# Probabilities times values in three passes of split parts, and VectorE's program woven unit by unit, in two attentions

## The chip, the cores and the metric

The kernel runs on one core of a Trainium2 chip. The metric is the device time of one execution in microseconds (us). A program has five engines that run their own instruction lists and meet at semaphores: TensorE (PE in the rows, with its weight loads as PEld), VectorE (DVE), ScalarE (ACT), GpSimd (POOL), and SyncE (SP), which only issues transfers here.

## The reference

Two transformer-like blocks run one after the other over 1024 tokens of width 1024. The change touches only their two attentions. In the first block ("fox") there are 8 heads of width 64 over 1040 positions (16 learnt ones ahead of the tokens), a causal mask and a bias per key:

```
s = jnp.einsum('bhqd,bhkd->bhqk', qi, kh, preferred_element_type=jnp.float32) * scale
s = s + Fi[..., None] - F[:, :, None, :]
s = jnp.where(kpos[None, :] <= pi[:, None], s, -jnp.inf)
p = jax.nn.softmax(s, axis=-1)
return jnp.einsum('bhqk,bhkd->bhqd', p.astype(vh.dtype), vh)
```

In the second ("mla") there are 16 heads with queries and keys of width 96 and values of width 64 over 1024 positions, and a mask by chunks of 64:

```
s = jnp.einsum('bqhd,bkhd->bhqk', qb, k[:, :k_end]).astype(jnp.float32) * scale
s = jnp.where(mask, s, -jnp.inf)
p = jax.nn.softmax(s, axis=-1).astype(v.dtype)
outs.append(jnp.einsum('bhqk,bkhd->bqhd', p, v[:, :k_end]))
```

Everything is float32. Around the attentions stand projections, a pooling and a convolution mixer, a recurrent branch and two mixtures of experts, which take most of the time and are left as they are.

## The kernel before, in words

Both attentions are the function `attention` (L976). A head is cut into **units**: one unit is 128 keys against up to 512 queries of one half of the sequence. The mla attention has 12 units a head: 512, 384, 256 and 128 queries for half 0, then five of 512 and 384, 256, 128 for half 1. The fox attention has 14: 512, 400, 272, 144, 16 for half 0, then five of 512 and 400, 272, 144, 16. For u, the number of the unit in its head, every engine has its own list.

**TensorE** holds two units of scores ahead. Its loop does, per unit u, the scores of u + 2 (L122: three products of split parts, high by high, low by high, high by low, with the mask added at L1189), then two pieces of the next head's row maxima (L1161, mask at L1164) while u is small, and last the product of unit u with the values, `fox_out` or `mla_out` (L1202). That product has float32 operands; the others have operands of the type fp32r, which are the rounded parts of a float32 number: the high part is a rounded copy, the low part is the value less the high part. The scores have three banks (R_S), the probabilities three buffers (R_P), the maxima two banks (R_M). At the head's first unit TensorE waits for the row of maxima, the copied values and the low parts.

**ScalarE** takes the exponential of every unit (L1257), copies finished sums out (L1245, after unit 1 for the half before and two units after the end of half 0), and after unit 7 (HIGH_AT) makes the high parts of the queries and keys of the head after next (L1239, two casts).

**VectorE** works head by head: it reduces all of the next head's maxima (L1276), joins and negates them (L1281), copies the turned row (L1285), inverts sums (L1064) and scales finished halves (L1069). The scaling reads two tensors in on-chip memory (SBUF); the inverse sums come to it by a transfer to DRAM and a spreading transfer back, both issued by SyncE (`inverse_of`).

**GpSimd** makes the low parts of queries and keys (L1131, two subtractions of 1024 or 1040 columns) once the scores of the head two before are done, and copies the values of a head to a buffer with a column of ones (L1123, one copy for each 128 keys).

**SyncE** loads the queries and keys of head h + 2 when the low parts of head h are there, and moves the sums, the inverses and the row of maxima. `Handover` (L957) holds the buffers that the stage behind the attention uses too.

## Time and profile before

| | us |
|---|---|
| median of 3 runs | 2957.4 |
| lowest, highest | 2955.4, 2964.36 |
| the profiled execution, its own time | 2955.65 |
| its span in the profile | 2953.9 |
| fox attention, from its first memory fill to its last copy out | 306.6 to 492.4 |
| mla attention, the same | 1668.7 to 1991.2 |

The two attentions are some 510 us of the span. Over the whole span TensorE is busy for 2664.0 us (90%), VectorE 1490.2 (50%), ScalarE 1113.5 (38%) and GpSimd 812.7 (28%). In the rows each operation has its line in the kernel before, its output and inputs, and its shape; "idle before" is the time its engine stood still ahead of it and what ended that. A TensorE record's duration overlaps with the next one's, so what a product costs is read from the distance between starts.

### The profile page before, as it was taken

To read this page: it belongs to the slowest core of one execution; us is meant where nothing else is said; L and a number is where in the kernel's file an instruction comes from. 1 tells how busy PE (TensorE), PEld (TensorE's weight loads), DVE (VectorE), ACT (ScalarE), POOL (GpSimd) and SP (SyncE) were. 2 spreads that over 40 slices of the span, in tenths; PEclk is the share of its full clock that TensorE was granted. 3 is DMA by queue.
4 is the path that set the end of the run, shared out by engine and by line. 5 is a ranking of instruction groups with operands and counts; after the bars stand their busy time and mean duration, and the time that the engine had idled before them with its cause. 6 is when DMAs were issued, how large, how long until landed. Compare 5 with 4: busy or idle time off the path is not lost. (4 is left out here: it accounts for less than half of the span.)

```text
span 2953.9 us, 34232 instructions
## 1 busy us (share of the span) xinstructions
PE 2664.0 (90%) x12244; PEld 2034.3 (69%) x12244; DVE 1490.2 (50%) x1840; ACT 1113.5 (38%) x1461; POOL 812.7 (28%) x685
## 2 busy tenths in 40 slices
PE   4999899999999799958999799999999989699887
PEld 3899566677668677746777455557777868677665
DVE  4196342222123578855466544433542443677775
ACT  3011443000012377752344344441332232377775
POOL 1242332212122133312100233323332312134444
PEclk7999899999999799978899899999999999799998
DMA  3110112111105487842522233332111123598985
GB/s 95 30 50 22 33 43 63 43 43 50 36 22 179 170 286 231 273 131 86 213 64 65 75 84 75 74 86 67 50 36 50 50 94 123 194 329 305 320 321 185
DMA packets 209415, 350.52 MB, mean 119 GB/s; under 512 B 40376, under 2 KB 159496, under 8 KB 189608
## 3 DMA queue, kind: packets, MB, share of 16 engines
q1 hardware_dynamic: 191824, 315.60, 32.0%
q0 software_dynamic: 17280, 33.60, 4.9%
q8 instruction: 56, 0.92, 0.1%
q14 instruction: 39, 0.32, 0.0%
q10 hardware_dynamic: 216, 0.07, 0.0%
HBM read 326.80 MB, written 72.48 MB: 135 GB/s over the span
## 5 line engine op out<-in xcount | busy, mean ns | idle before, releaser
L2078 DVE TENSOR_TENSOR moe_run_w_low_up<-moe_run_w,moe_run_w_high_up 128x2048 fp32r<-128x2048 f32 x116 | 265.4, 2289 | 127.7 <-ACT moe_run_w_high_up L1911 118.6
L1911 ACT CAST moe_run_w_high_up<-moe_run_w 128x2048 fp32r<-128x2048 f32 x116 | 221.2, 1906 | 114.1 <-DMA moe_run_w<-w_gate 63.9
L1848 PE MATMUL moe_run_up<-moe_run_w_high_up,moe_run_xT_high 128*128 128x512 f32 x464 | 192.6, 415 | 14.0 <-issue 13.7
L1848 PE MATMUL moe_run_up<-moe_run_w_low_up,moe_run_xT_high 128*128 128x512 f32 x464 | 184.0, 397 | 0.0
L1848 PE MATMUL moe_run_up<-moe_run_w_high_up,moe_run_xT_low 128*128 128x512 f32 x464 | 183.9, 396 | 0.0
L1394 DVE TENSOR_TENSOR merge_gated<-merge_branch,merge_gate 128x512 f32<-128x512 f32 x48 | 33.2, 691 | 280.9 <-ACT merge_gate L1378 280.7
L1257 ACT ACTIVATE mla_probs<-mla_scores 128x512 f32<-128x512 f32 x192 | 94.1, 490 | 174.6 <-PE mla_scores L1189 91.6
L1378 ACT ACTIVATE merge_gate<-merge_gates 128x512 f32<-128x512 f32 x48 | 28.7, 598 | 347.2 <-PE merge_branch L122 347.2
L1202 PE MATMUL mla_out<-mla_probs,mla_v 128*65 128x512 f32 (+3 forms) x384 | 150.4, 487 | 0.0
L134 PE MATMUL moe_run_down<-moe_run_w_high_down,moe_run_hT_high 128*128 128x512 f32 x232 | 98.3, 424 | 39.7 <-issue 36.0
L2078 DVE TENSOR_TENSOR moe_run_w_low_down<-moe_run_w,moe_run_w_high_down 128x2048 fp32r<-128x2048 f32 x58 | 132.3, 2281 | 0.0
L1276 DVE TENSOR_REDUCE mla_piece_max<-mla_max 128x1 f32<-128x512 f32 (+1 forms) x192 | 98.9, 550 | 60.4 <-PE mla_max L1161 41.2
L1848 PEld LDWEIGHTS moe_run_up<-moe_run_w_high_up,moe_run_xT_high 128*128 128x128 f32 x464 | 88.1, 190 | 46.5 <-issue 29.4
L122 PE MATMUL merge_branch<-features,merge_wy 128*128 128x512 f32 x256 | 117.7, 592 | 0.0
L134 PE MATMUL merge_gates<-uT_high,merge_wg_high 128*128 128x512 f32 x256 | 113.7, 444 | 0.0
L1918 ACT CAST moe_run_w_high_down<-moe_run_w 128x2048 fp32r<-128x2048 f32 x58 | 110.4, 1903 | 1.2 <-DMA moe_run_w<-exp_w 0.6
L1766 POOL DMA_INDIRECT out<-moe_run_y,moe_run_rows x34 | 58.3, 1715 | 179.8 <-DMA out<-moe_run_y,moe_run_rows 137.8
L134 PE MATMUL rnn_ps<-uT_again_high,mla_q_hi_then_high 128*128 128x512 f32 x256 | 102.2, 399 | 5.4 <-ACTq L2233 5.4
L1756 POOL DMA_INDIRECT moe_run_x<-v,moe_run_rows x58 | 91.7, 1580 | 49.9 <-POOL moe_run_rows L1792 44.8
L134 PE MATMUL proj_acc<-uT_high,proj_w_high 128*128 128x512 f32 (+2 forms) x272 | 97.1, 357 | 8.3 <-DVEq L559 8.2
L1848 PEld LDWEIGHTS moe_run_up<-moe_run_w_high_up,moe_run_xT_low 128*128 128x128 f32 x464 | 87.7, 189 | 21.2
L134 PE MATMUL rnn_ps<-uT_again_high,rnn_w_high 128*128 128x512 f32 x256 | 101.2, 396 | 0.0
(556 smaller groups left out, 7401.2 us busy)
## 6 DMA issues: line engine op xcount, KB each, us to landing
moe_run_w<-exp_w SPq DMA_DIRECT2D x72, 1024.0 KB
moe_run_w<-w_gate SPq DMA_DIRECT2D x34, 1024.0 KB
moe_run_w<-w_up SPq DMA_DIRECT2D x34, 1024.0 KB
moe_run_w<-w_down SPq DMA_DIRECT2D x34, 1024.0 KB
out_h<-x SPq DMA_DIRECT2D x16, 512.0 KB, 4.5
v<-out_v SPq DMA_DIRECT2D x16, 512.0 KB, 2.9
mla_raw_q_then_weights<-w_in SPq DMA_DIRECT2D x16, 512.0 KB, 3.9
rnn_raw<-w_in SPq DMA_DIRECT2D x16, 512.0 KB
```

The source lines that it names most:

```text
L122: last = pe.matmul(out, lhsT, rhs, start=(n == 0), stop=(n == len(pairs) - 1))
L134: last = pe.matmul(out, a, b, start=(k == 0), stop=(k == n - 1))
L1202: pe.matmul(ps_o[n][0:DH + 1, first - a:b - a], v_aug[h % 2][0:rows, t, :], probs[g % R_P][0:rows, first - a:b - a], start=(t == 0), stop= ...
L1257: act.activation(probs[g % R_P][0:rows, first - a:b - a], ps_s[g % R_S][0:rows, first - a:b - a], ACT.Exp).then_inc(s_exp, 1)
L1276: dve.tensor_reduce(pm[:, i, n:n + 1], ps_m[g % R_M][:, 0:b - a], AX.X, ALU.max).then_inc(s_mxfree, 1)
L1394: dve.tensor_tensor(pr[b][:], ps_y[b][:], sg[b][:], ALU.mult).then_inc(s_done, 1)
L1756: pool.indirect_dma_start(out=x[p][:], out_offset=None, in_=v_d, in_offset=bass.IndirectOffsetOnAxis(ap=rows[p][:, 1:2], axis=0), bounds_c ...
L1766: pool.indirect_dma_start(out=h_d, out_offset=bass.IndirectOffsetOnAxis(ap=rows[p][:, 0:1], axis=0), in_=y[p][:], in_offset=None, bounds_c ...
L1848: last = pe.matmul(up[p][:], a, w, start=(h == 0 and k == 0), stop=(h == 1 and k == 3 * HK - 1))
L1911: act.copy(hi[p][j], raw[p][j][:]).then_inc(s_hi[j], 1)
L1918: act.copy(hi[p][2], raw[p][2][:]).then_inc(s_hi[2], 1)
L2078: dve.tensor_tensor(lo[p][j], raw[p][j][:], hi[p][j].bitcast(F32), ALU.subtract).then_inc(s_lo[j], 1)
```

## The change

The product of probabilities and values is made in three passes of split parts, as the scores are.

- Values: GpSimd makes `v_hi` (a cast) and `v_lo` (a subtraction) for a head, each over all tiles at once, in place of 8 or 9 copies.
- Probabilities: behind every exponential ScalarE waits for it and makes `probs_hi`; VectorE then makes `probs_lo`, which lies over `probs` (`over`: two names for one place). TensorE waits for the first before its first two passes and for the second before its third.
- Queries and keys: the low part lies over the raw part. There are three such buffers, used in turn. GpSimd makes a head's low parts as soon as ScalarE has made the high ones; it no longer waits for the scores of an earlier head. ScalarE makes the high part of the queries after unit 7 and of the keys after unit 9.
- VectorE's list is woven: in each unit first `probs_lo`, then two maxima of the next head, and at set units the joining, the turned row, the inverses and the scalings.
- The constant rows are filled by VectorE (`s_const`), zeros in the low rows by GpSimd; SyncE waits for the scores of the head before in place of the low parts.

```diff
-    HIGH_AT = 7
-    INV1_AT = NM // 2
+    HIGH_AT = (7, 9)
+    LAST_MAX = FIRST + -(-NM // PER_UNIT) - 1
+    SCALE0_AT, INV1_AT, SCALE1_AT, INV0_AT = 1, 3, 8, ends[0] + 6
...
-                        sp.wait_ge(s_lo, 2 * h + 2)
-                        load_head(sp, p, h // 2 + 1, raw[p][0], raw[p][1], s_load[p])
+                        if h:
+                            sp.wait_ge(s_sc, NU * h)
+                        else:
+                            sp.wait_ge(s_init, 3)
+                        load(h + 2)
...
+                def split_v(h):
                     if h >= 2:
                         pool.wait_ge(s_pv, NU * (h - 1))
-                    for t in range(NK):
-                        rows = min(P, T - P * t)
-                        last = pool.tensor_copy(v_aug[h % 2][0:rows, t, 0:DH], v[0:rows, t, h * DH:(h + 1) * DH])
+                    high, low = v_hi[h % 2], v_lo[h % 2]
+                    for rows, tiles in ((P, slice(0, full)),) + (((rest, slice(full, NK)),) if rest else ()):
+                        src = v[0:rows, tiles, h * DH:(h + 1) * DH]
+                        own(pool.tensor_copy(high[0:rows, tiles, 0:DH], src))
+                        last = pool.tensor_tensor(low[0:rows, tiles, 0:DH], src,
+                                                  high[0:rows, tiles, 0:DH].bitcast(F32), ALU.subtract)
                     last.then_inc(s_v[h % 2], 1)
 
                 def split_low(h):
-                    if h >= 2:
-                        pool.wait_ge(s_sc, NU * (h - 1))
-                    for n, rows in enumerate((one_row, k_all)):
+                    for n, rows in enumerate((dq, one_row)):
                         pool.wait_ge(s_hi, 2 * h + n + 1)
...
-                    pe.wait_ge(s_exp, g + 1)
-                    pe.matmul(ps_o[n][0:DH + 1, first - a:b - a], v_aug[h % 2][0:rows, t, :],
-                              probs[g % R_P][0:rows, first - a:b - a],
-                              start=(t == 0), stop=True, skip_group_check=True).then_inc(s_pv, 1)
+                    pe.wait_ge(s_ph, g + 1)
+                    out, at = ps_o[n][0:DH + 1, first - a:b - a], slice(first - a, b - a)
+                    vh, vl = (w[h % 2][0:rows, t, :] for w in (v_hi, v_lo))
+                    ph, pl = (w[g % R_P][0:rows, at] for w in (p_hi, p_lo))
+                    pe.matmul(out, vh, ph, start=(t == 0), stop=False, skip_group_check=True)
+                    pe.matmul(out, vl, ph, start=False, stop=False, skip_group_check=True)
+                    pe.wait_ge(s_pl, g + 1)
+                    pe.matmul(out, vh, pl, start=False, stop=True, skip_group_check=True).then_inc(s_pv, 1)
...
                                        ps_s[g % R_S][0:rows, first - a:b - a], ACT.Exp).then_inc(s_exp, 1)
+                        act.wait_ge(s_exp, g + 1)
+                        act.copy(p_hi[g % R_P][0:rows, first - a:b - a],
+                                 probs[g % R_P][0:rows, first - a:b - a]).then_inc(s_ph, 1)
...
-                        if u == HIGH_AT and h + 2 < heads:
-                            split_high(h + 2)
+                        if u in HIGH_AT and h + 2 < heads:
+                            split_high(h + 2, HIGH_AT.index(u))
...
+                def rest_of_probs(h, u):
...
+                    dve.wait_ge(s_ph, g + 1)
+                    dve.tensor_tensor(p_lo[g % R_P][0:rows, first - a:b - a], probs[g % R_P][0:rows, first - a:b - a],
+                                      p_hi[g % R_P][0:rows, first - a:b - a].bitcast(F32),
+                                      ALU.subtract).then_inc(s_pl, 1)
...
                 for h in range(heads):
-                    if h + 1 < heads:
-                        maxima_of(h + 1)
-                    else:
-                        invert(dve, h - 1, 1)
-                    if h:
-                        scale_out(dve, h - 1, 1)
-                    invert(dve, h, 0)
-                    scale_out(dve, h, 0)
+                    for u in range(NU):
+                        rest_of_probs(h, u)
+                        if h + 1 < heads:
+                            for m in range(PER_UNIT * (u - FIRST), PER_UNIT * (u - FIRST + 1)):
+                                if 0 <= m < NM:
+                                    max_of(h + 1, m)
```

VectorE's list in an mla head was, before (`mla_sums` are the sums to be inverted, `oT` the finished output):

```order
L1276 TENSOR_REDUCE mla_piece_max<-mla_max 128x1 x7
L1064 RECIPROCAL mla_sums<-mla_sums 128x4
L1276 TENSOR_REDUCE mla_piece_max<-mla_max 128x1 x5
L1281 TENSOR_REDUCE mla_neg_max<-mla_piece_max 128x8
L1285 CAST mla_neg_rows<-mla_turned 8x128
L1069 TENSOR_TENSOR oT<-mla_unscaled,oT 64x512
L1064 RECIPROCAL mla_sums<-mla_sums 128x4
L1069 TENSOR_TENSOR oT<-mla_unscaled,oT 64x512
```

The last row stood ahead of the next head's maxima. From unit 5 to the end of the head VectorE's list is now this (`mla_probs_lo` with a number of its own for each of the three buffers):

```order
L1315 TENSOR_TENSOR mla_probs_lo_11617<-mla_probs,mla_probs_hi 128x512
L1296 TENSOR_REDUCE mla_piece_max<-mla_max 128x1 x2
L1301 TENSOR_REDUCE mla_neg_max<-mla_piece_max 128x8
L1315 TENSOR_TENSOR mla_probs_lo_11615<-mla_probs,mla_probs_hi 128x512
L1315 TENSOR_TENSOR mla_probs_lo_11616<-mla_probs,mla_probs_hi 128x512
L1307 CAST mla_neg_rows<-mla_turned 8x128
L1315 TENSOR_TENSOR mla_probs_lo_11617<-mla_probs,mla_probs_hi 128x512
L1078 TENSOR_TENSOR oT<-mla_unscaled,oT 64x512
L1315 TENSOR_TENSOR mla_probs_lo_11615<-mla_probs,mla_probs_hi 128x384
L1073 RECIPROCAL mla_sums<-mla_sums 128x4
L1315 TENSOR_TENSOR mla_probs_lo_11616<-mla_probs,mla_probs_hi 128x256
L1315 TENSOR_TENSOR mla_probs_lo_11617<-mla_probs,mla_probs_hi 128x128
```

A subtraction stands in every unit, and the scaling of half 1 in unit 8; the scaling of half 0 moved to unit 1 of the next head.

ScalarE's list in an mla head, from unit 7 on, before:

```order
L1257 ACTIVATE mla_probs1<-mla_scores1 128x512
L1239 CAST mla_q_hi_then_high<-mla_raw_q_then_weights 96x1024
L1239 CAST mla_k_hi_then_low<-mla_k0 97x1024
L1257 ACTIVATE mla_probs2<-mla_scores2 128x512
L1257 ACTIVATE mla_probs0<-mla_scores0 128x384
L1257 ACTIVATE mla_probs1<-mla_scores1 128x256
L1257 ACTIVATE mla_probs2<-mla_scores2 128x128
```

The same place in the changed program:

```order
L1274 ACTIVATE mla_probs1<-mla_scores1 128x512
L1277 CAST mla_probs_hi1<-mla_probs1 128x512
L1254 CAST mla_q_hi_then_high<-mla_q2 96x1024
L1274 ACTIVATE mla_probs2<-mla_scores2 128x512
L1277 CAST mla_probs_hi2<-mla_probs2 128x512
L1274 ACTIVATE mla_probs0<-mla_scores0 128x384
L1277 CAST mla_probs_hi0<-mla_probs0 128x384
L1254 CAST mla_k_hi_then_low<-mla_k2 96x1024
L1274 ACTIVATE mla_probs1<-mla_scores1 128x256
L1277 CAST mla_probs_hi1<-mla_probs1 128x256
L1274 ACTIVATE mla_probs2<-mla_scores2 128x128
L1277 CAST mla_probs_hi2<-mla_probs2 128x128
```

Every exponential has a cast behind it, and the cast of the keys moved to behind unit 9. GpSimd's subtractions of the same head are issued right behind these two casts, in units 7 to 11, and its list for a head is now:

```order
L1147 TENSOR_TENSOR mla_q_lo2_11613<-mla_q2,mla_q_hi_then_high 96x1024
L1147 TENSOR_TENSOR mla_k_lo2_11614<-mla_k2,mla_k_hi_then_low 96x1024
L1139 CAST mla_v_hi0<-v2_tokens 128x8x64
L1140 TENSOR_TENSOR mla_v_lo0<-v2_tokens,mla_v_hi0 128x8x64
L1147 TENSOR_TENSOR mla_q_lo0_11610<-mla_q0,mla_q_hi0 96x1024
```

Before, the first two rows ran at the start of a head, behind the scores of the head before, and eight copies stood in place of the third and fourth.

## Rows read from the trace of the kernel before

**Rows 1.** Busy time of each engine in three stretches of one head: fox, mla, mla
```profile
core 0: us, PE busy (x) PEld busy (x) DVE busy (x) ACT busy (x) POOL busy (x), PEclk, DMA share, GB/s
344.30:365.20 20.90, 20.14 (x106) 12.86 (x104) 9.73 (x19) 9.14 (x19) 6.78 (x11) 1.00 0.17 39
1762.30:1781.70 19.40, 18.38 (x90) 11.37 (x89) 8.32 (x18) 8.60 (x17) 6.59 (x10) 1.00 0.37 109
1744.30:1763.37 19.07, 18.35 (x90) 11.36 (x89) 8.03 (x18) 8.64 (x17) 6.57 (x11) 1.00 0.28 57
```
**Rows 2.** Timeline of TensorE in an mla head: start us, us, operation
```profile
1764.66 0.40 PE L122 MATMUL mla_scores<-mla_q_lo,mla_k_hi 97*128 97x512 f32 x1
1764.89 0.40 PE L122 MATMUL mla_scores<-mla_q_hi,mla_k_lo 97*128 97x512 f32 x1
...
1778.45 1.02 PE L1202 MATMUL mla_out<-mla_probs,mla_v 128*65 128x512 f32 x2
1778.91 0.74 PE L122 MATMUL mla_scores<-mla_q_hi,mla_k_hi 97*128 97x384 f32 x1
1779.48 0.34 PE L122 MATMUL mla_scores<-mla_q_lo,mla_k_hi 97*128 97x384 f32 x1
1779.66 0.34 PE L122 MATMUL mla_scores<-mla_q_hi,mla_k_lo 97*128 97x384 f32 x1
```
**Rows 3.** Waits of TensorE for VectorE, mla then fox: us, times, longest
```profile
PE mla_max L1161 <- DVE mla_piece_max L1276: 11.4, 14, 1.0
PE fox_max L1161 <- DVE fox_piece_max L1276: 5.0, 6, 0.9
```
**Rows 4.** Groups of ScalarE by shape: exponentials and casts, busy us, mean ns
```profile
L1257 ACT ACTIVATE mla_probs<-mla_scores 128x512 f32<-128x512 f32 x87 | 51.9, 596 | 105.3 <-PE mla_scores L122 75.2 <-PE mla_scores L1189 28.5
L1257 ACT ACTIVATE mla_probs<-mla_scores 128x384 f32<-128x384 f32 x30 | 14.7, 490 | 11.0 <-PE mla_scores L1189 10.2
L1239 ACT CAST mla_k_hi<-mla_k 97x1024 fp32r<-97x1024 f32 x9 | 9.4, 1045 | 0.0
L398 ACT CAST uT_high<-norm_turn 128x512 fp32r<-128x512 f32 x32 | 17.6, 579 | 6.1 <-PE norm_turn L460 5.9
```
**Rows 5.** Groups of VectorE by shape: maxima, fox scalings, two-input operations elsewhere
```profile
L1276 DVE TENSOR_REDUCE mla_piece_max<-mla_max 128x1 f32<-128x512 f32 x86 | 57.9, 688 | 38.4 <-PE mla_max L1161 38.4
L1069 DVE TENSOR_TENSOR features<-fox_unscaled,features 64x512 f32<-64x512 f32 x14 | 19.0, 1359 | 44.0 <-DMA features<-fox_inverse 43.9
L447 DVE TENSOR_TENSOR uT_low<-norm_turn,uT_high 128x512 fp32r<-128x512 f32 x32 | 20.7, 683 | 1.6 <-ACT uT_high L398 1.6
L2657 DVE TENSOR_TENSOR qkv_q<-qkv_q,latent_squares 128x256 f32<-128x256 f32 x8 | 3.4, 425 | 0.3
```
**Rows 6.** Timeline of GpSimd and VectorE: the scaling beside GpSimd's subtraction, and alone
```profile
455.75 2.42 POOL L1131 TENSOR_TENSOR fox_k_lo<-fox_k,fox_k_hi 66x1040 fp32r<-66x1040 f32 x1
455.85 2.87 DVE L1069 TENSOR_TENSOR features<-fox_unscaled,features 64x512 f32<-64x512 f32 x1 [4.92 <-DMA features<-fox_inverse]
...
1785.10 2.36 POOL L1131 TENSOR_TENSOR mla_k_lo<-mla_k,mla_k_hi 97x1024 fp32r<-97x1024 f32 x1
1786.73 1.28 DVE L1069 TENSOR_TENSOR oT<-mla_unscaled,oT 64x512 f32<-64x512 f32 x1 [5.30 <-DMA oT<-mla_inverse]
...
1799.46 0.67 DVE L1069 TENSOR_TENSOR oT<-mla_unscaled,oT 64x512 f32<-64x512 f32 x1
```
**Rows 7.** Groups of GpSimd: subtractions in mla and in the recurrent branch, copied values
```profile
L1131 POOL TENSOR_TENSOR mla_k_lo<-mla_k,mla_k_hi 97x1024 fp32r<-97x1024 f32 x9 | 21.2, 2361 | 0.0
L147 POOL TENSOR_TENSOR rnn_w_low<-rnn_raw,rnn_w_high 128x1024 fp32r<-128x1024 f32 x16 | 49.7, 3106 | 1.3
L1123 POOL COPY mla_v<-v_tokens 128x64 f32<-128x64 f32 x112 | 27.2, 291 | 0.0
```
**Rows 8.** Timeline from an inverse to its scaling: VectorE, SyncE's issue, VectorE
```profile
1761.62 0.16 DVE L1064 RECIPROCAL mla_sums<-mla_sums 128x4 f32<-128x4 f32 x1
1763.37 0.47 SPq L1059 DMA_DIRECT2D oT<-mla_inverse  x1
1767.99 0.80 DVE L1069 TENSOR_TENSOR oT<-mla_unscaled,oT 64x512 f32<-64x512 f32 x1 [6.22 <-DMA oT<-mla_inverse]
```
**Rows 9.** Busy time in stretches of 20 us in the expert stages, columns as in rows 1
```profile
1140.00:1160.00 20.00, 16.51 (x65) 12.88 (x64) 14.80 (x12) 11.82 (x11) 6.04 (x5) 0.83 0.80 263
2820.00:2840.00 20.00, 16.53 (x73) 12.44 (x73) 15.55 (x12) 13.61 (x13) 8.69 (x6) 1.00 0.91 324
```

137 lines of the change are left out of this document (86 added, 51 removed).

## The prediction

> **What bounds the kernel now.** I first cut one head out of each attention and read each engine's busy time [rows 1]. A fox head takes 20.9 us, an mla head 19.07 or 19.40, 19.2 in the mean. TensorE is busy for all but about 1 us of it, with the granted clock at 1.00; ScalarE and VectorE work 8 to 10 us of 19 to 21, GpSimd under 7. So TensorE's list sets a head's length. The one hole in it is a wait of up to 1.0 us a head for a bank of maxima [rows 3]: VectorE stands at the scaling of a finished half, whose inverse is still on its way [rows 8], and the maxima are queued behind it. The change takes work from TensorE and puts new work on the three others; the question is whether TensorE still sets the pace.
>
> **TensorE.** From the timeline [rows 2]: a pass of 512 fp32r columns starts 0.23 us after the last (1764.66 to 1764.89), one of 384 after 0.18. The float32 product of 512 columns starts at 1778.45; the scores behind it reach their second pass at 1779.48, so their first, of 0.18, ran from 1779.30, and the product held the array 0.85 us. Three passes take 3 x 0.233 = 0.70: 0.15 saved on each of 6 units of 512, 0.1 and 0.07 on the two units each of 384 and 256, and about 0.1 lost on the two of 128, where three passes of about 0.1 (weight loads set them) replace 0.21. That is 0.9 + 0.2 + 0.14 - 0.2 = 1.05 us less in an mla head, and by the same count 0.8 in a fox head. With the wait of rows 3 gone too (0.8 us a head in either), TensorE alone would need about 17.4 us for mla and 19.3 for fox.
>
> On this point the Trainium skill can be weighed against the row. FP8 and Floating Point Precision, section TensorE Precision Notes, says that true FP32 takes four passes through the array. The 0.85 us are four times 512 columns at the granted full clock, so it agrees; by it, with passes of equal length, the saving would be 0.21 for a unit of 512 and some 7 us more over all 24 heads than I count. The row's 0.233 for an fp32r pass decides.
>
> **ScalarE.** An exponential of 512 columns is 0.60 us, of 384 0.49 [rows 4], by their slope 0.39 for 256 and 0.28 for 128: 5.9 us an mla head. The cast behind each is not in the trace in that shape. From on-chip memory 1024 columns take 1.045, and 512 columns from a bank 0.579 [rows 4]; I take 0.60, 0.49, 0.39, 0.28, another 5.9 us. With two copies out (0.58 each) and two casts of queries and keys (1.04 each) the list is 15.05 us, and 0.5 for the waits on itself (12 x 0.04, an estimate): 15.5. It can start 1.06 us into the head (first scores 0.83, handover 0.23) and I count 1.5 us in which it waits for scores, because TensorE stands two units ahead at most. It ends at 18.1; the last subtraction of 128 columns (0.29), two passes and their handovers bring the head to **19.0 us**. That is 0.2 under 19.2. For fox the same list (12.7 + 3.2 + 0.6 us) gives **20.2**, 0.7 under 20.9. So even undisturbed most of what TensorE saves is lost, at the end of each head, where exponential, cast, subtraction and product of four narrowing units stand in a row and the next head's scores are queued behind the last product.
>
> **VectorE.** The subtraction is bounded by 0.683 us (512 columns, one input from a bank) and by 0.425 for 256 from on-chip memory [rows 5]: 0.69, 0.56, 0.43, 0.29, some 0.07 less when back to back, some 6 us an mla head. A maximum of 512 is 0.69, all twelve 5.9. From the first subtraction's end (3.0 us into the head) VectorE needs for units 0 to 6: maxima 5.9, subtractions 3.6, one scaling 0.65, joining and inverse 0.3, with small waits for banks to 13.4 us, where TensorE would want unit 6 at about 13.2. So it is level until there.
>
> **GpSimd, the term that decides.** Look at the scaling, the one VectorE operation before with both inputs in on-chip memory [rows 6]. Alone it takes 0.67 us. At 455.85 it meets GpSimd's subtraction (455.75 to 458.17) and takes 2.87: it ends 0.55 after GpSimd. At 1786.73 it meets one that ends at 1787.46 and ends 0.55 after that. It stands still until GpSimd is through. The fourteen fox scalings of that stretch take 1.36 us in the mean [rows 5]; every second one meets GpSimd. `probs_lo` has the same form, and there are 12 or 14 a head. The other way round GpSimd waits too: its subtraction, 2.36 alone, takes 3.11 in the recurrent branch [rows 7]. Before, the two subtractions of 2.36 us stood at a head's start, and met one scaling. Now they follow the casts behind units 7 and 9, where VectorE has no maxima left and TensorE waits for each subtraction.
>
> A head of mla, laid out in that way: the cast of the queries ends at 13.2 (ScalarE's list to unit 7). GpSimd waits for unit 6's subtraction to end at 13.4, then holds until 15.8. Unit 7's is through at 16.4; TensorE wanted it at 14.9. The keys' cast ends at 16.6 and GpSimd takes its second 2.4 us at once or one operation later; either way VectorE then has to fit 2.4 of waiting, unit 8 (0.62), the scaling (0.65), unit 9 (0.5), the inverse (0.15), unit 10 (0.4) and unit 11 (0.28) behind 16.4: 21.4, and with the last pass **21.7 us**, +2.5 on 19.2. Fox: 16.3 + 2.4 + 0.62 + 0.65 + 0.62 + 0.15 + 1.42 (units 10 to 13) + 0.3 = **22.5**, +1.6 on 20.9. The last two heads of each attention have no such casts. The values' cast and subtraction (some 1.9 us from rows 7's rates, against 8 x 0.29 of copies) run at a head's start, before the first subtraction, and cost nothing unless the head before ran late.
>
> The same rule stands in the Trainium skill, SBUF - State Buffer, section SBUF: two separate sides: the port pair that VectorE and GpSimd share is held for a whole instruction, also between a VectorE operation with two SBUF inputs and a GpSimd one that reads SBUF, and the other blocks. By it the sum is the one below; read as mere sharing of bandwidth, rows 6 would give about half the delay, near 2976.
>
> **The small rest.** VectorE fills three rows (mla) or six (fox) before the first cast, unseen in the trace; the cast anyway waits some 6 us for its load: 0 to 3 us in all, I take 1. SyncE's loads wait for the same moment as before within 1 us and land ten units early: nothing. The last head's inverse is taken at unit 9 or 10 and needs 6.4 us to its scaling [rows 8], 1 us later than before for each attention: 2.
>
> **The sum.** 14 x 2.5 = 35.0, the two last mla heads -0.7, 6 x 1.6 = 9.6, the two last fox heads -1.4, and 3 of rest: +45.5 us. On the profiled execution's 2955.65 (span 2953.9, median of the runs 2957.4) that is 3001; I say 3002.
>
> **Rivals.**
> 1. Only one of GpSimd's two subtractions costs time, because the other falls beside maxima or an idle VectorE: about half the delay, 14 x 1.15, 6 x 0.5, less 2.1, and the 3 of rest: +20: 2976. For it: my layout puts the first only 0.5 us behind the last maxima.
> 2. GpSimd's share is hidden or VectorE wins the port: heads of 19.0 and 20.2, 16 x -0.2, 8 x -0.7, +3: 2950, on the edge of what can be told. Against it stand rows 6 and the fox mean of rows 5.
> 3. Faster: TensorE stays the bound, since casts and handovers are cheaper than I take them. Heads of 17.4 and 19.3: 16 x -1.8, 8 x -1.6, + 3: -39, 2917. It needs the four narrow units to follow each other within TensorE's own time; in units 10 and 11 one exponential, cast and subtraction come to 1.2 and 0.85 us against passes of 0.36 and 0.3, which speaks against it. It decides if ScalarE's list ends before 16.5 us.
> 4. Worse: with the inverse of half 0 taken at 21 us, its scaling (6.4 us later) is due 5.7 us into the next head, where VectorE comes to it at about 5.4; behind it maxima and subtractions stop. And TensorE would be busy under 80% of a head: at 16.5 of 20 us the granted clock was once 1.00 and once 0.83 [rows 9]. Either adds 1 us a head: 3026.
>
> **Chances.** Forecast 0.50, rival 1 0.14, rival 2 0.14, rival 3 0.14, rival 4 0.08. A difference under 0.3% (2948.5 to 2966.3) can't be told from none. Slower: 0.50 + 0.14 + 0.08 = 0.72; rival 2 straddles the edge, 0.09 same and 0.05 faster; with rival 3 faster is 0.19. The range takes in the forecast and rivals 1 and 2: 2942 to 3025, leaving 0.2 outside.
>
> **What would show it.** In the profile after: `probs_lo` of 512 columns with a median of 0.65 to 0.7 and a maximum near 3 us, the long ones in units 7 to 11; an mla head of 21 to 22 us with TensorE waiting for VectorE before the third pass; product passes 0.23 us apart; casts of 0.6. If no subtraction of probabilities is longer than 1 us, the deciding term is wrong; if heads are 19 us long, it was hidden.

## The result, and the profile after

The changed kernel takes 3047.3 us (median of 4 runs, 3044.5 to 3060.5; a fifth on record, outside that median, took 3039.5), the kernel before 2960.4 beside it: a ratio of 1.0296 [1.0261, 1.0331], 87 us more. Forecast were 3002, 45 more, and a range up to 3025. The sign and GpSimd's hold on VectorE were right. The price was half of what it is, because the sum had no term for TensorE's clock. The profiled execution is the slowest of the four, 3060.5, and 104.9 over the profiled one before, so its rows overstate the median by up to 13 us.

Busy time of each engine over the span of 3058.8 us, from the page of the changed kernel, and its row of the granted clock in 40 slices:

```profile
PE 2737.2 (89%) x12548; PEld 2123.3 (69%) x12548; DVE 1695.7 (55%) x2161; ACT 1256.7 (41%) x1765; POOL 860.7 (28%) x547
...
PEclk9999867999999799969899788879999999799999
```

The new work stands on VectorE (+205 us) and ScalarE (+143). TensorE, which was to lose work, is busy 73 us longer. A busy TensorE is not a fast one: in the 40 slices the clock row falls to 8, 6 and 7 inside fox (slices 5 to 7) and lies at 7 to 8 across mla (23 to 27).

From the first memory fill to the last copy out fox now takes 225.3 us (185.8 before) and mla 393.2 (322.5 before): +39.5 and +70.7, all of the loss; everything else together is 5 us shorter. The next view answers [rows 1]: busy time of each engine in stretches of the changed kernel, five fox heads in a row, two mla heads in a row, and a piece of the last mla head. Columns as there; the column after the POOL counts is the granted clock.

```profile
core 0: us, PE busy (x) PEld busy (x) DVE busy (x) ACT busy (x) POOL busy (x), PEclk, DMA share, GB/s
342.07:363.90 21.83, 19.46 (x119) 13.80 (x118) 16.68 (x34) 15.31 (x33) 7.07 (x6) 1.00 0.16 35
363.90:386.49 22.59, 20.75 (x118) 14.67 (x117) 17.07 (x35) 15.34 (x33) 7.06 (x7) 0.92 0.17 40
386.49:416.54 30.05, 27.25 (x112) 19.86 (x110) 17.35 (x34) 15.54 (x32) 7.08 (x6) 0.64 0.13 28
416.54:447.54 31.00, 29.87 (x118) 21.36 (x118) 16.85 (x35) 15.55 (x32) 8.56 (x7) 0.61 0.13 27
447.54:480.22 32.68, 30.39 (x118) 22.00 (x118) 16.94 (x35) 15.52 (x32) 7.45 (x7) 0.60 0.11 25
1789.20:1812.50 23.30, 20.43 (x102) 14.46 (x101) 17.10 (x31) 14.42 (x29) 7.16 (x4) 0.85 0.20 48
1812.50:1837.00 24.50, 21.72 (x102) 15.16 (x101) 17.20 (x32) 14.50 (x29) 7.15 (x5) 0.79 0.33 87
2075.00:2092.00 17.00, 16.71 (x93) 11.61 (x93) 9.77 (x21) 13.53 (x29) 0.00 (x0) 1.00 0.20 42
```

Read the fox rows downwards. VectorE, ScalarE and GpSimd have the same lists in every head. The first two heads take 21.8 and 22.6 us at clocks of 1.00 and 0.92, beside a forecast of 22.5. The next three take 30 to 33, with a clock near 0.6 and TensorE "busy" for all but 1 to 3 us. The mla heads are 23.3 and 24.5 in turn, 23.9 in the mean, at 0.85 and 0.79; forecast 21.7.

The timeline of GpSimd, VectorE and TensorE in one mla head shows how the two things hang together (start us, us, engine, line, operation; in brackets the wait before it). L1315 is `probs_lo`, L1147 GpSimd's subtraction, L1218 TensorE's third pass:

```profile
1789.21 2.93 POOL L1147 TENSOR_TENSOR mla_q_low<-mla_raw_q_then_weights,mla_q_hi 96x1024 fp32r<-96x1024 f32 x1 [14.19 <-ACT mla_q_hi L1254]
...
1790.73 1.97 DVE L1315 TENSOR_TENSOR mla_probs_lo<-mla_probs,mla_probs_hi 128x512 fp32r<-128x512 f32 x1
...
1792.47 2.44 POOL L1147 TENSOR_TENSOR mla_k_lo<-mla_k,mla_k_hi 96x1024 fp32r<-96x1024 f32 x1 [0.33 <-ACT mla_k_hi L1254]
1792.72 2.73 DVE L1078 TENSOR_TENSOR oT<-mla_unscaled,oT 64x512 f32<-64x512 f32 x1
...
1792.75 0.45 PE L1218 MATMUL mla_out<-mla_probs_lo,mla_v_hi 128*65 128x512 f32 x1 [0.67 <-DVE mla_probs_lo L1315]
...
1795.48 0.56 DVE L1315 TENSOR_TENSOR mla_probs_lo<-mla_probs,mla_probs_hi 128x384 fp32r<-128x384 f32 x1
...
1796.10 0.39 PE L1218 MATMUL mla_out<-mla_probs_lo,mla_v_hi 128*65 128x384 f32 x1 [2.19 <-DVE mla_probs_lo L1315]
```

GpSimd's first subtraction ends at 1792.14 and VectorE's at 1792.70; the second ends at 1794.91 and VectorE's scaling at 1795.45. Both times VectorE ends 0.55 us after GpSimd, the signature of [rows 6], twice in each head. The first hold costs TensorE 0.67 us. What was not in the forecast is that the long wait falls on the scaling: `probs_lo` of unit 9 is queued behind it and TensorE has a hole of 2.19 us. Then the clock answers. TensorE's passes behind that hole, and the clock in the two stretches:

```profile
1801.06 0.63 PE L1216 MATMUL mla_out<-mla_probs_hi,mla_v_lo 128*65 128x512 f32 x1
1801.49 0.63 PE L1218 MATMUL mla_out<-mla_probs_lo,mla_v_hi 128*65 128x512 f32 x1
...
1804.69 0.40 PE L122 MATMUL mla_scores<-mla_q_hi,mla_k_hi 97*128 97x512 f32 x1
1804.92 0.39 PE L122 MATMUL mla_scores<-mla_q_lo,mla_k_hi 97*128 97x512 f32 x1
```
```profile
1797.70:1804.60 6.90, 6.90 (x28) 5.22 (x28) 2.98 (x6) 3.91 (x9) 1.19 (x2) 0.51 0.50 136
1789.20:1797.70 8.50, 5.63 (x34) 3.73 (x34) 6.73 (x9) 4.26 (x9) 5.97 (x3) 1.00 0.03 6
```

Passes of 512 columns start 0.43 us apart and later 0.23 again: the lower level of the clock (1.2 GHz) and the upper (2.4). In the 8.5 us with the holes TensorE worked 5.63 at the full clock; the 6.9 us behind them ran at 0.51. In fox the lower level lasts longer, with TensorE busy throughout:

```profile
394.90:422.20 27.30, 27.30 (x97) 19.90 (x95) 12.29 (x28) 12.43 (x27) 4.63 (x5) 0.50 0.14 29
422.20:429.00 6.80, 5.67 (x38) 4.03 (x37) 4.84 (x8) 3.84 (x10) 4.31 (x2) 1.00 0.03 3
429.00:452.90 23.90, 23.90 (x81) 17.09 (x80) 12.01 (x26) 11.41 (x23) 4.25 (x5) 0.50 0.16 34
```

The groups by shape answer [rows 4] and [rows 5] (count, busy us, mean ns, idle before):

```profile
L1315 DVE TENSOR_TENSOR mla_probs_lo<-mla_probs,mla_probs_hi 128x512 fp32r<-128x512 f32 x96 | 82.0, 867 | 58.0 <-ACT mla_probs_hi L1277 58.0
L1277 ACT CAST mla_probs_hi<-mla_probs 128x512 fp32r<-128x512 f32 x96 | 59.6, 620 | 3.0
L1078 DVE TENSOR_TENSOR oT<-mla_unscaled,oT 64x512 f32<-64x512 f32 x32 | 49.9, 1560 | 8.6 <-DMA oT<-mla_inverse 8.0
```

The cast is 0.62 us (taken as 0.60). The subtraction has a mean of 0.87, against 0.69 in the sum, and the scaling 1.56, where it takes 0.67 alone.

### The profile page after: what moved, and what is told of

The parts are those of the page before. It is cut to its first block and busy times, and to the rows that moved or that the text cites. A ratio compares the mean times of both kernels' runs of the same rounds, so it can differ in the third digit from the quotient of the medians.

```text
span 3058.8 us, 35307 instructions
## 1 busy us (share of the span) xinstructions
PE 2737.2 (89%) x12548; PEld 2123.3 (69%) x12548; DVE 1695.7 (55%) x2161; ACT 1256.7 (41%) x1765; POOL 860.7 (28%) x547
## 5 line engine op out<-in xcount | busy, mean ns | idle before, releaser
L1902 PE MATMUL moe_run_up<-moe_run_w_high_up,moe_run_xT_high 128*128 128x512 f32 x464 | 193.5, 417 | 21.6 <-issue 21.4
L1315 DVE TENSOR_TENSOR mla_probs_lo<-mla_probs,mla_probs_hi 128x512 fp32r<-128x512 f32 x192 | 125.3, 665 | 58.9 <-ACT mla_probs_hi L1277 58.5
L1810 POOL DMA_INDIRECT moe_run_x<-v,moe_run_rows x58 | 115.8, 1996 | 50.2 <-POOL moe_run_rows L1846 37.2
L1218 PE MATMUL mla_out<-mla_probs_lo,mla_v_hi 128*65 128x512 f32 x192 | 74.7, 390 | 41.0 <-DVE mla_probs_lo L1315 40.7
L1902 PEld LDWEIGHTS moe_run_up<-moe_run_w_high_up,moe_run_xT_low 128*128 128x128 f32 x464 | 87.9, 189 | 21.2
```

Source lines behind the costliest of these rows:

```text
L1218: pe.matmul(out, vh, pl, start=False, stop=True, skip_group_check=True).then_inc(s_pv, 1)
L1315: dve.tensor_tensor(p_lo[g % R_P][0:rows, first - a:b - a], probs[g % R_P][0:rows, first - a:b - a], p_hi[g % R_P][0:rows, first - a:b - a ...
L1810: pool.indirect_dma_start(out=x[p][:], out_offset=None, in_=v_d, in_offset=bass.IndirectOffsetOnAxis(ap=rows[p][:, 1:2], axis=0), bounds_c ...
L1902: last = pe.matmul(up[p][:], a, w, start=(h == 0 and k == 0), stop=(h == 1 and k == 3 * HK - 1))
```

## The experiments

The question is which part of the 87 us is GpSimd's hold on VectorE, which the clock, and which the added work as such. The program outside the two attentions, which no run edits, takes 2440 to 2457 us in the thirteen profiled executions, so it alone can move a total by 16 us. I therefore read **head lengths** beside the medians: the distance between the casts of two heads' queries on ScalarE, as a mean over the 13 mla and 5 fox distances from the third such cast on, in the profiled execution.

| kernel | mla head | fox head | median us | ratio to before [95%] |
|---|---|---|---|---|
| before | 19.2 | 20.9 | 2954 to 2960 | 1 |
| changed | 23.9 | 27.6 | 3047.3 | 1.0296 [1.0261, 1.0331] |
| GpSimd fills zeros | 18.8 | 19.6 | 2946.2 | 0.9958 [0.9941, 0.9974] |
| idle products, 9 a head | 21.5 | 25.0 | 3022.6 | 1.0217 [1.0197, 1.0237] |
| the same, 4 a head in fox | 21.6 | 23.6 | 3017.1 | 1.0211 [1.0183, 1.0238] |
| low parts on VectorE | 19.9 | 22.6 | 2983.2 | 1.0098 [1.0076, 1.012] |
| low parts a few units later | 25.5 | 31.6 | 3111.9 | 1.0531 [1.0499, 1.0563] |
| low parts in pieces | 21.2 | 24.6 | 3009.3 | 1.0195 [1.0164, 1.0227] |
| float32 product back | 18.1 | 19.8 | 2934.3 | 0.9925 [0.99, 0.9949] |
| the same, low parts later | 18.1 | 19.8 | 2934.2 | 0.9932 [0.9911, 0.9954] |
| zeros, no cast | 19.0 | 19.3 | 2942.4 | 0.996 [0.9947, 0.9974] |
| the same, later inverses | 18.5 | 18.7 | 2942.4 | 0.9963 [0.995, 0.9977] |
| zeros, later inverses | 18.8 | 19.3 | 2950.3 | 0.9992 [0.9981, 1.0002] |

"Before" was run again beside each group of runs, and the ratios are to those runs. The answer in short, in medians: the woven list alone gains some 24 us; the three passes with their casts and subtractions, GpSimd's zeros in place of its work, take some 12 of that back; GpSimd's subtractions, with what the clock does behind them, cost 101, of which idle products in TensorE's hole give back 25 to 30 by keeping the clock up.

### Without GpSimd's subtractions

```diff
-                        pool.tensor_tensor(lo[h % R_L][n][0:rows, :], raw[h % R_L][n][0:rows, :],
-                                           hi[h % R_H][n][0:rows, :].bitcast(F32), ALU.subtract).then_inc(s_lo, 1)
+                        if h >= 2:
+                            pool.memset(lo[h % R_L][n][0:rows, :].bitcast(F32), 0.0).then_inc(s_lo, 1)
+                            continue
...
```

> The changed kernel, but from head 2 on GpSimd fills the low parts of queries and keys with zeros (0.95 us each, nothing read from on-chip memory) in place of subtracting (2.4 us each, two inputs read). So the low parts' share of the scores is left out; every wait and every other instruction stays. Theory A (the port that GpSimd and VectorE share opens a hole at each head's end, and the hole halves TensorE's clock behind it): no subtraction of probabilities above 1 us in units 7 to 11, clock 1.00 in mla, heads of 19 to 19.5 us against 23.9, some 2945 to 2960 us in all. Theory B (the row of exponential, cast, subtraction and third pass is itself too long, and the clock falls for that): heads stay at 22 us or more, over 3010.

Measured 2946.2, within the expectation: 101 us come back, and the heads are 18.8 and 19.6 against 19.0 and 20.2 forecast for heads without the port's price. Two mla heads in windows, the groups, and a fill beside a subtraction (timeline):

```profile
1754.17:1773.11 18.94, 18.16 (x102) 12.23 (x101) 13.61 (x31) 14.20 (x29) 3.71 (x5) 1.00 0.34 106
1773.11:1791.16 18.05, 17.99 (x102) 12.30 (x101) 13.73 (x32) 14.20 (x29) 3.71 (x5) 1.00 0.26 62
```
```profile
L1318 DVE TENSOR_TENSOR mla_probs_lo<-mla_probs,mla_probs_hi 128x512 fp32r<-128x512 f32 x96 | 64.0, 679 | 48.0 <-ACT mla_probs_hi L1280 48.0
...
L1078 DVE TENSOR_TENSOR oT<-mla_unscaled,oT 64x512 f32<-64x512 f32 x32 | 21.8, 682 | 8.1 <-DMA oT<-mla_inverse 7.7
```
```profile
1790.55 1.28 DVE L1318 TENSOR_TENSOR mla_probs_lo<-mla_probs,mla_probs_hi 128x512 fp32r<-128x512 f32 x2
1791.16 0.95 POOL L1148 MEMSET mla_q_low<- 96x1024 f32 x1 [10.91 <-ACT mla_q_hi L1257]
```

The subtraction is back at 0.68 us in the mean and the scaling too, and the clock is at 1.00 in both windows. A fill of 0.95 us beside two subtractions costs them nothing (1.28 for two): what blocks is GpSimd's subtraction, not GpSimd being at work.

### Holding TensorE busy across the hole

```diff
+                    if u == NU - 3 and h + 2 < heads:
+                        keep_busy(pe, cst, ps_m[0], 9)
                     pe.wait_ge(s_pl, g + 1)
```

`keep_busy` issues products of a constant with itself into a free bank; nothing reads them.

> The changed kernel with nine idle products (512 bf16 columns each, into a bank of maxima that is free there) ahead of the third pass of the third last unit of each head, where TensorE stands still for 2.2 us. All work of the reference is done. Theory A with the clock as a term of its own: VectorE is as late as before, so the head ends at the same point, but the granted clock no longer falls behind the hole; mla heads 21.5 to 22 us against 23.9, the slow stretch in fox gone, 2995 to 3010 in all: what I had forecast without the clock. If the clock is no term of its own, the time stays within 10 us of the changed kernel or grows.

Measured 3022.6: added work made the kernel 25 us faster. GpSimd's subtractions and their hold on VectorE are as they were; idle products stand in the hole, and the clock stays up. Windows of 20 us in mla:

```profile
1740.00:1760.00 20.00, 19.21 (x109) 12.49 (x107) 16.20 (x29) 14.29 (x28) 7.17 (x4) 1.00 0.24 54
1760.00:1780.00 20.00, 17.47 (x100) 11.86 (x100) 15.41 (x28) 13.81 (x26) 5.58 (x4) 1.00 0.38 107
```

The mla head is 21.5, which is the 21.7 of the forecast, made for the full clock. The total is 13 us above the range that I expected. One reason is that in fox nine products are too many, and the heads are 25.0. A second run had four of them in fox:

> The changed kernel with idle matrix products ahead of the third pass of the unit before the last three, as in the run with 9 of them a head, but with 4 a head in fox (9 in mla, as there). All arithmetic is there. With 9 the fox heads took 24.5 us where I forecast 22.5 for a head with the port's price and full clock; in it one row of nine took 3.8 us. Theory A (the filler itself was too long for fox, the clock is the rest): fox heads of 22.5 to 24 us, mla heads as there at 21.5, 3008 to 3018 us in all. Rival B (in fox the clock falls whenever the hole is not filled whole): fox heads go back towards 30 us with a granted clock near 0.5 to 0.6, 3035 to 3060. If the fox heads stay at 24.5 with the clock at 1.00, my 22.5 was too low by 2 us for another reason.

Measured 3017.1, within the expectation. That is 5 us less, with runs of the two kernels that overlap; the fox heads say it more clearly, 23.6 us, two of them in windows:

```profile
389.42:412.81 23.39, 20.26 (x122) 14.13 (x121) 17.30 (x35) 15.35 (x33) 7.10 (x7) 1.00 0.16 35
412.81:436.31 23.50, 20.26 (x122) 14.10 (x121) 17.35 (x35) 15.34 (x33) 7.09 (x6) 1.00 0.15 34
```

Beside the changed kernel's 30 to 33 us for the same heads this is the clock's own price: some 2.3 us of an mla head and 4.0 of a fox head (27.6 less 23.6) in the mean, 9 in the worst. By heads that is 56 us over both attentions. The medians are 30 us apart and the ratios 25. The spans of the profiled executions are 42 apart: the two attentions are 58 us shorter, the program outside them is 16 us longer (2456.4 against 2440.3), and the changed kernel's profiled execution lies 13 over its median. So the clock's share is 25 to 30 of the 87 us by the medians, and some 56 in the profiled execution. What the idle products themselves cost is in both.

What lowers the clock is not shown by this. In the timeline of this run the fox heads in mid-stage still have two holes of 1.3 to 1.5 us each, and four of the five head lengths are at a clock of 1.00; in the changed kernel holes of that length stood ahead of the 27 us at the lower level. Idle products at one point of the head were enough, and these runs do not say why.

### Moving the subtractions

Low parts made by VectorE, behind units 7 and 9, GpSimd's left out for heads from the third on:

```diff
+                        if u in HIGH_AT and h + 2 < heads:
+                            low_of(h + 2, HIGH_AT.index(u))
```

> The changed kernel with the low parts of queries and keys (heads 2 on) made by VectorE, behind units 7 and 9 of its list, 1.2 us each, in place of GpSimd's 2.4. All work of the reference is done. Theory A: no hole above 1 us, clock mostly 1.00, mla heads 19.2 to 20.3 us, 2950 to 2980 in all. Theory B: VectorE's extra 2.4 us and the long row at the head's end leave heads at 21 us or more, over 3000.

Measured 2983.2, 3 over theory A's range: 64 us better than on GpSimd. The same subtraction takes VectorE 1.20 us, and nobody is blocked by it, but it stands in VectorE's list; mla heads are 19.9 at full clock. Fox heads vary from 19.8 to 26.3 with a clock of 0.86 over 340 to 440 us. There the clock stood at the lower level for 27.3 us, though no hole in the 50 us before was longer than 0.5. So the fall needs neither these subtractions on GpSimd nor a long hole.

The old place of the subtractions, on GpSimd:

```diff
                 def split_low(h):
+                    if h >= 2:
+                        pool.wait_ge(s_sc, NU * (h - 1))
```

> One change to the changed kernel: GpSimd's two subtractions of queries and keys wait again for the scores of the head two before, so that they run at a head's start as in the kernel before, and no longer behind units 7 and 9. All arithmetic is there. Theory A (a VectorE subtraction stands still until GpSimd is through, and where it stands decides the price; TensorE's idle time then halves its clock): the two now meet units 0 and 1 of the next head, where TensorE holds scores and maxima ahead and VectorE is not yet behind, but the first third pass comes up to 4 us late. I expect the long probs_lo in units 0 to 2, one hole of some 2 to 3 us at the head's start, mla heads of 20.5 to 22.5 us against 23.9, and 2975 to 3020 us in all. Rival B (the amount of work on ScalarE and VectorE sets the head, wherever GpSimd's work stands): within 0.3% of the changed kernel, about 3047. Rival C (only the place was wrong, and at the head's start all of it is hidden): heads as with GpSimd's work left out, 18.8 us, about 2946.

Measured 3111.9, slower than all three theories said. The timeline of one head shows my error:

```profile
1822.98 2.36 POOL L1149 TENSOR_TENSOR mla_q_low<-mla_raw_q_then_weights,mla_q_hi 96x1024 fp32r<-96x1024 f32 x1 [17.79 <-PE mla_scores L1201]
1823.08 0.34 PE L1220 MATMUL mla_out<-mla_probs_lo,mla_v_hi 128*65 128x384 f32 x1
1823.37 4.60 DVE L1317 TENSOR_TENSOR mla_probs_lo<-mla_probs,mla_probs_hi 128x256 fp32r<-128x256 f32 x2 [0.35 <-ACT mla_probs_hi L1279]
1825.29 2.54 POOL L1149 TENSOR_TENSOR mla_k_lo<-mla_k,mla_k_hi 96x1024 fp32r<-96x1024 f32 x1
...
1825.67 0.33 PE L1220 MATMUL mla_out<-mla_probs_lo,mla_v_hi 128*65 128x256 f32 x1 [1.83 <-DVE mla_probs_lo L1317]
...
1828.03 0.28 PE L1220 MATMUL mla_out<-mla_probs_lo,mla_v_hi 128*65 128x128 f32 x1 [1.90 <-DVE mla_probs_lo L1317]
```

TensorE makes scores two units ahead, so "when a head's scores are done" falls in unit 9 of that head and not at the start of the next. Both subtractions run back to back beside the subtractions of units 10 and 11: two of them, some 0.7 us of work, take 4.6. TensorE stands 1.83 and 1.90 us within 3 us, with nothing ahead to do. The same GpSimd work in another place costs 65 us more, the clock's part in it (0.80 in nearly every mla head) included: the price is set by what VectorE holds up, as the forecast reasoned, and the forecast's phrase "at a head's start" for the kernel before was loose.

Each subtraction cut into pieces of 256 columns, place unchanged:

```diff
+                        for c in range(0, w, 256):
+                            b = w if c + 256 >= w else c + 256
+                            last = pool.tensor_tensor(lo[...][0:rows, c:b], raw[...][0:rows, c:b], ...)
```

> One change to the changed kernel: each of GpSimd's subtractions of queries and keys is cut into pieces of 256 columns (four or five instructions in a row in place of one). Same columns, same place behind units 7 and 9. Theory A (the port is held for one instruction, and VectorE gets in between two): a probs_lo waits at most for one piece, some 0.6 to 0.7 us, its maximum falls from 2.7 to about 1.4 us, GpSimd's own work gets longer by the time VectorE takes in between, TensorE has no hole above 1 us and keeps its full clock; mla heads of 19 to 20.5 us, 2950 to 2990 us in all. Rival B (GpSimd keeps the port from one of its instructions to the next while it has work queued): long probs_lo as before, time within 0.5% of the changed kernel or longer by the extra instructions, 3045 to 3070. Rival C (VectorE and GpSimd share bandwidth): cutting changes nothing, 3047.

Measured 3009.3, between the theories. Timeline of one head, then two heads in windows:

```profile
1779.23 4.22 POOL L1150 TENSOR_TENSOR mla_q_lo<-mla_q,mla_q_hi_then_high 96x256 fp32r<-96x256 f32 x4 [10.50 <-ACT mla_q_hi_then_high L1258]
...
1780.73 0.98 DVE L1319 TENSOR_TENSOR mla_probs_lo<-mla_probs,mla_probs_hi 128x512 fp32r<-128x512 f32 x1
...
1781.64 1.22 DVE L1078 TENSOR_TENSOR oT<-mla_unscaled,oT 64x512 f32<-64x512 f32 x1
```
```profile
1779.23:1799.52 20.29, 18.17 (x102) 12.20 (x101) 16.26 (x31) 14.19 (x29) 9.35 (x10) 1.00 0.37 99
1843.10:1866.81 23.71, 22.25 (x102) 15.59 (x101) 15.96 (x32) 14.35 (x29) 9.28 (x11) 0.78 0.22 46
```

VectorE gets in between two pieces: 0.98 and 1.22 us in place of 1.97 and 2.73, while GpSimd's four pieces take 4.22 in place of 2.93. The longest subtraction of probabilities beside pieces is 1.23 us in either attention; the two of 2.4 that remain stand beside whole subtractions of the stage that follows. So the hold lasts one instruction. The port's price fell to what was expected (20.3 us at a clock of 1.00), but some heads of the same execution, with the same work on every engine, ran 23.7 at 0.78. The clock's price did not go with the long holes. In the timeline of these heads TensorE's holes are 0.90 and 0.76 us without a fall and 0.92 and 0.93 with one, and each fall lasted 10.2 us. A remedy that halves the hole can still leave the fall.

### The woven list alone

The float32 product put back, with neither casts nor subtractions of probabilities and values; the woven list, low parts in place and GpSimd's early subtractions stay:

```diff
-                    pe.wait_ge(s_ph, g + 1)
...
-                    pe.matmul(out, vh, ph, start=(t == 0), stop=False, skip_group_check=True)
-                    pe.matmul(out, vl, ph, start=False, stop=False, skip_group_check=True)
-                    pe.wait_ge(s_pl, g + 1)
-                    pe.matmul(out, vh, pl, start=False, stop=True, skip_group_check=True).then_inc(s_pv, 1)
+                    pe.wait_ge(s_exp, g + 1)
+                    pe.matmul(out, vh, probs[g % R_P][0:rows, at],
+                              start=(t == 0), stop=True, skip_group_check=True).then_inc(s_pv, 1)
```

> The changed kernel with the float32 product of probabilities and values back: no rounded probabilities or values, no casts and subtractions for them; VectorE's woven list, low parts in place, three load buffers and GpSimd's early subtractions stay. All work of the reference is done. Theory A: GpSimd's subtractions then meet only the scaling, TensorE never waits for that, mla heads lose part of the 0.8 us wait at maxima and take 18.5 to 19.2 us: 2935 to 2960. Theory C (the moved list of VectorE or the moved loads are what costs): it is slower than the kernel before, over 2975.

Measured 2934.3, just under theory A's range, and with its sister below the fastest of all. Two mla heads in windows:

```profile
1750.32:1768.39 18.07, 18.07 (x90) 11.28 (x90) 8.07 (x19) 8.68 (x16) 5.33 (x4) 1.00 0.40 117
1768.39:1786.41 18.02, 18.02 (x90) 11.27 (x90) 8.17 (x19) 8.68 (x16) 5.33 (x3) 1.00 0.23 59
```

TensorE is busy without a gap: 1.1 us less a head in both attentions than before, where the wait of [rows 3] alone was 0.8. With GpSimd's subtractions back at their old place on top:

> The kernel with the float32 product put back (no splits of probabilities and values; VectorE's list woven, low parts in place), and on top GpSimd's two subtractions again at a head's start, as in the kernel before. What is left of the change against the kernel before is the weaving of VectorE's list, ScalarE's key cast behind unit 9, the values copied in one instruction, and low parts in place. Against the woven kernel with the early subtractions (2934.3 us, ratio 0.9925): if the gain is the weaving (TensorE's wait for maxima gone), within 0.3% of it, 2928 to 2943. If the gain came from GpSimd's earlier subtractions (TensorE waits for low parts at a head's start before), it falls back to about 2950 to 2960. Without probs_lo there is nothing of VectorE's with two SBUF inputs but the scalings, so the port should not matter in either.

Measured 2934.2 (6 runs): the same. The gain is not in the placement of the subtractions, and without `probs_lo` their place costs nothing. Weaving is the one change left that touches the wait for maxima, which makes it the likely cause; the copy of values in one instruction, low parts in place and the later cast of the keys were not run by themselves, and 0.3 us of the 1.1 is more than that wait.

### What holds an undisturbed head

The forecast said that ScalarE's list sets it. On top of the zeros, the exponential writes the rounded probabilities itself:

```diff
-                        act.activation(probs[...], ps_s[...], ACT.Exp).then_inc(s_exp, 1)
-                        act.wait_ge(s_exp, g + 1)
-                        act.copy(p_hi[...], probs[...]).then_inc(s_ph, 1)
+                        act.activation(p_hi[...], ps_s[...], ACT.Exp).then_inc(s_ph, 1)
```

> The kernel in which GpSimd writes zeros in place of the low parts of queries and keys, with one more thing left out: ScalarE's exponential writes the rounded probabilities itself and the cast behind it is gone (5.9 us of an mla head's list by my count); VectorE's subtraction stays in length and place, but subtracts the rounded part from itself. So the low share of queries, keys and probabilities is left out. It asks what holds that kernel's heads at 18.8 us where TensorE alone would need 17.4 by my count. Theory A (ScalarE's list and the chain exponential, cast, subtraction of the narrow units): heads fall to TensorE's own length, 17.2 to 17.8 us mla and 19.0 to 19.5 fox, TensorE waits for nothing over 0.3 us, 2910 to 2925 us in all. Rival B (VectorE's woven list alone is as long or comes too late: maxima 5.9, subtractions 5.6, scalings 1.3 and small ones, 13.5 us and up): heads stay within 0.4 us of 18.8, 2935 to 2946. Rival C (the three passes cost more than 0.70 us a unit beside the weight loads, so that 18.8 is TensorE's own length): TensorE's busy share near 100% and 2940 or more.

Measured 2942.4, rival B: with some 6 us of ScalarE's work gone from every head, mla heads are 19.0 in the mean against 18.8, fox 19.3 against 19.6. ScalarE's list did not set them. They vary from 17.0 to 22.3, and the timeline of one long one says what came last:

```profile
1767.27 0.18 DVE L1073 RECIPROCAL mla_sums<-mla_sums 128x4 f32<-128x4 f32 x1 [2.04 <-DMA mla_sums<-mla_unscaled]
1767.37 0.66 DVE L1315 TENSOR_TENSOR mla_probs_lo<-mla_probs_hi 128x512 fp32r<-128x512 f32 x1
...
1768.09 0.44 PE L1221 MATMUL mla_out<-mla_probs_lo,mla_v_hi 128*65 128x512 f32 x1 [1.81 <-DVE mla_probs_lo L1315]
```

VectorE stands at the inverse for a transfer, and the subtraction is queued behind it. So I moved these points back:

```diff
-    SCALE0_AT, INV1_AT, SCALE1_AT, INV0_AT = 1, 3, 8, ends[0] + 6
+    SCALE0_AT, INV1_AT, SCALE1_AT, INV0_AT = 2, 5, 10, ends[0] + 8
```

> The kernel without the cast of the probabilities and with GpSimd's zeros (low shares of queries, keys and probabilities left out), and one more edit: VectorE takes its inverses two units later (half 1 after unit 5 in place of 3, half 0 after the last unit in mla) and its scalings one or two units later. In the run before, mla heads were 17.2 and 19.4 us in turn; in a long one VectorE stood 2.04 us at the inverse of half 1 for the transfer of the sums, the subtraction of unit 4 was queued behind it, and TensorE waited 1.81 us for that. Theory A (that wait is what is left between 17.2 and 19.4): all mla heads 17.2 to 17.6 us, TensorE alone as I forecast it (17.4), fox 19.2 to 19.6, 2915 to 2928 us in all. Rival B (VectorE's load as such; the wait only shows who comes last): heads stay at 18.3 in the mean, 2938 to 2946.

Measured 2942.4, rival B, no change in the total; heads went from 19.0 to 18.5 and 19.3 to 18.7. That comparison leans to one side: the profiled execution without this edit was the slowest of its ten (2950.9), the one with it was an ordinary one (2942.2). Over 1740 to 1900 us VectorE's waits for the sums fell from 10.7 us to 0.4, and waits for the inverses at the scalings came up instead:

```profile
DVE oT L1078 <- DMA oT<-mla_inverse: 8.5, 8, 1.3
...
DVE mla_sums L1073 <- DMA mla_sums<-mla_unscaled: 0.4, 1, 0.4
```

The wait moved to the other end of the transfers, and TensorE still waits for `probs_lo`: 9.5 us in that stretch, 10.9 before. The same edit with the cast in place:

> The same later inverses and scalings in the kernel that still has ScalarE's cast behind every exponential (GpSimd's zeros stay; only the low shares of queries and keys are left out). Its mla heads were 18.8 us without this edit. Theory A of my prediction (ScalarE's list and the chain of the narrow units hold the undisturbed head): the edit gives little here, 18.3 to 18.8 us a head and 2935 to 2946 in all, while the kernel without the cast drops. Rival B (the inverses' wait held both): it drops with the other, to 17.2 to 17.8 us a head, 2915 to 2930.

Measured 2950.3, as theory A expected, a little above its range; mla heads 18.8 as without the edit. That is no proof of A, whose other half (the kernel without the cast drops) had failed. What these runs leave: TensorE alone needs 17.0 to 17.2 us (the shortest heads here), ScalarE's list is not what separates that from 18.8, and VectorE's order, with transfers and `probs_lo` in one queue, is in the chain. Which step of it is the last could not be settled.

## Why the prediction was right or wrong

- **TensorE's saving: right.** 17.4 us was the sum for mla, the shortest heads without other limits are 17.0 to 17.2. Against the float32 product with the same woven list (18.05) that is 0.85 to 1.05 us saved; the forecast had 1.05. Two of its terms were off and cancel: passes of 128 columns start about 0.06 us apart at the full clock, not 0.1, so nothing is lost on the units of 128, and the first pass of a 512 unit takes 0.26, so that such a unit saves 0.12 rather than 0.15. The Trainium skill (FP8 and Floating Point Precision, TensorE Precision Notes) has four passes for true FP32. If a pass of split parts were as long as one of them, a quarter of every product would be saved, 1.9 us an mla head and some 20 us more than forecast over the 24 heads (an estimate from the row's 0.85, scaled by columns; the forecast's "some 7 us" was added up wrongly, and nothing hung on it). The measurement decides for the row.
- **The undisturbed head: right in size, wrong in its reason.** 19.0 and 20.2 forecast, 18.8 and 19.6 measured. But ScalarE's list does not set it, since taking its casts away gave nothing in mla and 0.3 us in fox. The size was partly luck. I had added ScalarE's times up and never laid VectorE's list beside the transfers it waits for.
- **GpSimd's port: right.** The head with the port's price was put at 21.7 and 22.5. Measured at full clock: 21.5 for mla; 21.8 and 22.6 (clock 0.92) for the first two fox heads. The 0.55 us behind GpSimd's end and the maximum of `probs_lo` near 3 us (2.72 in mla) came as described. The layout was off by a unit: it had unit 7's subtraction held first, and measured it is unit 8's, then the scaling. The two waits of TensorE, 0.67 and 2.19 us, add up to 2.9, near the 2.7 between the forecast's heads of 19.0 and 21.7. The rule of the Trainium skill (SBUF - State Buffer, SBUF: two separate sides) that the pair is held for a whole instruction agrees with the pieces of 256 columns (1.23 us at most in place of 2.7). Mere sharing of bandwidth is out by that run, and rival 1, with only one of the two subtractions paid for, by the timeline and the head of 21.5.
- **The clock: the step that failed.** The sum holds every head at the full clock. Rival 4 had the clock in it, but priced it, like a late scaling, at 1 us a head, with a chance of 0.08 for the rival, from a pair of rows in the expert stages [rows 9] where the same busy time had once 1.00 and once 0.83. Measured are 2.3 us in an mla head and 4.0 in a fox head. Over 14 and 6 heads that is 32 + 24 = 56 us in the profiled execution (30 between the medians, 25 by the ratios), where 1 us a head gives 24. Its sign, "TensorE would be busy under 80% of a head", was wrong too: the mla heads at 0.79 and 0.85 are busy for 88 to 89%, fox heads at 0.60 to 0.64 for 91 to 96%, and one at 1.00 for 89%. A bound was in reach: passes of 512 columns are 0.43 us apart at the lower level and 0.23 at the upper, so a head with 17 us of matrix work loses 5 to 6 us if a third of that work is done there (an estimate; the third is an assumption). My range ended at 3025, where 1 us a head ends.
- **The rest.** Fills, later loads and the last inverse were put at 3 us. No run takes them apart. Rivals 2 and 3 fell with the port.
- **Together, against the forecast:** stage by stage fox is +39.5 where 8.2 was in the sum (six heads of 1.6, less 1.4), mla +70.7 where 34.3 was. In fox 24 of the 31 missing are the clock by the run with four idle products (6 x 4.0); its heads of 23.6 are 1.1 over the forecast's 22.5, and what that is stays open. In mla 14 x 2.2 = 31 of the 36 are the clock.

## What to carry to other kernels

When a change puts VectorE operations with two inputs from on-chip memory on a path that TensorE waits for, look for the GpSimd subtractions that run at the same time: each costs what is left of its own length, and what is queued behind VectorE pays it too. Then ask what TensorE's new holes do to the clock, and price the lower level as a term of its own, with a wide range: here it lasted 7 to 10 us at a stretch in the mla heads and 24 to 31 in the slow fox heads. Before rounding a product into three passes to save 0.15 us each, try what else the change brings alone: here the woven list without the three passes is 24 us faster than the kernel before. The three passes do not reach it in the total, even with GpSimd's subtractions left out. In the profiled executions the two attentions take 490 us with the woven list alone and 499 with passes and zeros; only with the cast left out and the inverses moved as well do they come to 486.

## What was not expected of the hardware

- A hole of 2.19 us at full clock was followed by about 7 us at 0.51, and nine idle products in the hole kept most heads at 1.00: a kernel with more work ran 25 us faster (3022.6 against 3047.3).
- In fox three heads in a row stood at 0.60 to 0.64 while TensorE was busy 91 to 96% of them, after two at 1.00 and 0.92 with the same program. The lower level lasted 27, 24 and 31 us at a stretch, with TensorE busy for all of it. Why it lasts longer there than in mla no run shows.
- The clock is not a plain function of a head's work: with GpSimd's work in pieces, one head took 20.29 us at 1.00 and another 23.71 at 0.78, with VectorE, ScalarE and GpSimd busy for nearly the same time. Nor is it one of the length of a hole: it fell behind holes of 0.9 us there and 0.45 with the low parts on VectorE, and stayed up through holes of 1.3 to 1.5 in the run with four idle products.
- A GpSimd fill beside VectorE's subtraction costs nothing; a GpSimd subtraction stops it until 0.55 us after its own end.
